# Four-quarter inverse products and an opening by token blocks in a hybrid mixer kernel

## The chip, the core and the metric

The kernel runs on one core of a Trainium2 chip. The metric is the device time of one execution in microseconds (us). A core has TensorE (PE: matmuls, with the weight loads shown apart as PEld), VectorE (DVE), ScalarE (ACT), GpSimd (POOL) and SyncE (SP, which here only issues DMAs). PE writes to PSUM, 8 banks of 512 fp32 numbers in each of 128 partitions.

## What is computed

One decoder layer over 512 tokens and 16 meta tokens, width 1024:

```python
h = (_rms(x, norm1_g[l]) * valid).astype(dt)
z = h @ w_in[l]
...
r, decay, k, v, kk, a, g = rwkv7_project(c_in, ...)
y_rw = rwkv7_mix(r, decay, k, v, kk, a, g, rw_rk[l], rw_ln_g[l], rw_ln_b[l])
...
merged = (gates[:, :, 0] * (y_sb.astype(dt) @ p_sb[l]) + ...)
x = x + (merged.astype(dt) @ w_o[l]).astype(dt)
h2 = _rms(x, norm2_g[l]).astype(dt)
x = x + squared_relu_mlp(h2, w_up[l], w_down[l]).astype(dt)
```

`rwkv7_mix` is a scan over the tokens, for 8 heads of 64 channels:

```python
S = (S * w_t[:, :, None, :]
     - jnp.einsum('bhij,bhj->bhi', S, kk_t)[..., None] * b_t[:, :, None, :]
     + v_t[..., None] * k_t[:, :, None, :])
```

## The kernel before

Every engine runs one hand-written program; semaphores order them (`wait_ge`, `then_inc`). Nothing is scheduled at run time.

**Dense work.** All large products are "jobs", in one list (`JOBS`). A job's weights come as units of 128 x 1024 numbers: SP loads a unit into `raw` (3 slots), ACT rounds it to the high part (`high`, `w_hi`, L784), POOL subtracts for the low part (`low`, `w_lo`, L667). The activations too are kept as high and low parts, and a product is three matmuls (`product3`, L1611 to L1613). A feature job over all 544 columns does them as two halves of 272 columns, for 8 slices `k` of the width each.

**Opening.** `x` arrives in four blocks of 128 tokens (`xt`) and the meta block (`xm`, 32 rows). ACT takes sums of squares and the scale of each block (L798 to L800), DVE multiplies by it (L1192). When all five blocks are scaled, PE turns them (L1650, L1653) for one slice `k` after the other, all blocks in a slice; ACT (L805, L806) and DVE (L1202, L1205) multiply the turned slice by the gain `norm1_g`, which lies along the partitions, and split it into `h_hi` and `h_lo`. Then the dense jobs begin, first the two of `PHASE_C[0]` and `PHASE_C[1]`; ACT copies the result of each (L820).

**RWKV part.** The scan is done for 32 meta tokens (block 0, one chunk of 32) and four blocks of 128 tokens, each two chunks of 64, whose rows stand in partitions 0 to 63 and 64 to 127. Within a chunk an inverse of a 64 x 64 triangle is built in 6 levels (5 in block 0) for each head. A level beyond the first is: PE `c1` products (L2055: `MM` by `TT`), ACT copy to `C1` (L1141), PE `u` products (L2064: `C1` by `XX`), DVE addition into `XX` (L1528), DVE transposition into `TT` (L1534); POOL masks the next `MM` (L744). Heads come in two groups `g` of four. Between `c1` and `u`, and between `u` and the next `c1`, PE does a piece of a dense job (`pieces(fill[...])`). After the levels come `F` products (L2073), their copy into `FK` (L1146), `wz` products (L2081), their copy (L1537) and the products of the state (L2096 to L2105); between these three `RW_FILL` has no pieces.

These products have 64 rows in and 64 out, so each uses one quarter of the PE array. The lines that say which:

```python
for h in range(4 * g, 4 * g + 4):
    o = CH * (h % 4)
    for rows, _, _ in chunks:
        last = M(pst[rows, 4 + 2 * g, o:o + m], MM[rows, step % 2, h, 0:m],
                 TT[rows, h, 0:m], start=True, stop=True)
```

The output partitions are the input's: chunk 0 uses the quarter (rows 0 to 63 in, 0 to 63 out), chunk 1 the one opposite. `c1` of group `g` goes to bank 4 + 2g, `u` to bank 5 + 2g. The products of the state (L2096 to L2105) already use all four quarters: either chunk's rows to either half of the output.

Of the kernel before, what the change touches and what calls it, by code (L numbers as in the profile page):

```python
# [6 lines left out]
ALU = mybir.AluOpType  # L7
ACT = mybir.ActivationFunctionType
# [5 lines left out]
P = 128  # L14
# [204 lines left out]
def build(nc, x, meta, weights, lora, consts, params, out):  # L219
    with ExitStack() as ctx:  # L220
# [35 lines left out]
        rs0 = place("rs0", [P, NB + 1], at=at)  # L256

# [146 lines left out]
        hn_ready = sem("hn_ready")  # L404
        ht_done = sem("ht_done")
# [3 lines left out]
        zeros_ready, cbuf_zeroed = sem("zeros_ready"), sem("cbuf_zeroed")  # L409
        c_copied, c_mixed = sem("c_copied"), sem("c_mixed")  # L410
        wa_tanh, sg_tanh, sg_ready = sem("wa_tanh"), sem("sg_tanh"), sem("sg_ready")
# [12 lines left out]
        f_done, f_copied, wz_done, wz_ready = sem("f_done"), sem("f_copied"), sem("wz_done"), sem("wz_ready")  # L424
# [17 lines left out]
        sb_diag_zeroed, sb_kmd_ready, sb_vmd_ready = sem("sb_diag_zeroed"), sem("sb_kmd_ready"), sem("sb_vmd_ready")  # L442
# [8 lines left out]
        rg_tanh, rqd_ready, rsz_zeroed = sem("rg_tanh"), sem("rqd_ready"), sem("rsz_zeroed")  # L451
# [38 lines left out]
        def halves(row):  # L490
            return row.rearrange("p (a b) -> p a b", a=2)

# [140 lines left out]
        def _(sp):  # L633
            for b in range(NB):
                if b == NB - 1:

                    sp.wait_ge(zeros_ready, 1)
                    sp.dma_start(xm[MB - N_META:MB, :], meta).then_inc(x_in, 16)
# [20 lines left out]
        def _(pool):  # L659
# [106 lines left out]
        def _(act):  # L766
# [36 lines left out]
            for k in range(KD):  # L803
# [3 lines left out]
                if k in (2, 4):  # L807
                    high(k // 2)
# [1394 lines left out]
```

## Time and profile before

| | |
|---|---|
| median of 3 runs | 1324.9 us (1324.51 to 1329.6) |
| the profiled execution's own time | 1325.9 us |
| its span in the profile | 1324.1 us |
| PE busy | 1234.7 us (93%) |
| chain that ended last | 77% PE |
| mean granted TensorE clock | 0.983 of full |

The profile shows one execution. A timeline row may merge several instructions of a line (xN), its duration then runs from the first's start to the last's end. A plain fp32 matmul leaves two records, so eight 64 x 64 products are 16 records.

### The profile page before, as it was taken

What the parts mean: (1) busy time and instruction counts of PE and PEld (TensorE: products, weight loads), DVE (VectorE), ACT (ScalarE), POOL (GpSimd) and SP (SyncE); (2) the same over time, 40 slices, a digit from 0 to 9 for tenths busy, and PEclk for the clock granted to TensorE, in tenths of its full rate; (3) what the DMA queues carried; (4) which work ended last, traced back from release to release, by engine and by line L of the source; (5) the groups of instructions that cost most, each with busy time, mean ns of one, the idle gap of its engine ahead of it and who ended that gap; (6) DMA issues with size and microseconds to landing.
All of it is one profiled execution on the core that took longest, in us unless ns stands there. A gap on an engine that the chain in (4) does not pass through costs nothing.

```text
span 1324.1 us, 21007 instructions
## 1 busy us (share of the span) xinstructions
PE 1234.7 (93%) x9042; PEld 1018.6 (77%) x9042; DVE 460.7 (35%) x834; ACT 492.7 (37%) x788; POOL 465.6 (35%) x287
## 2 busy tenths in 40 slices
PE   5999999899999989997999989888899999999998
PEld 4998878787889668765677767668788888788886
DVE  3599221323231452442243464453422200122000
ACT  5456322121222342776344543542533311133210
POOL 2443435232423224333232432233234544244541
PEclk9999999999999999999999999999999999999999
DMA  6212323121211132101421211141122232122330
GB/s 227 80 65 88 117 77 106 43 72 65 97 51 49 40 110 74 35 32 48 181 79 56 82 64 65 48 143 64 64 80 96 97 111 96 64 96 96 112 127 32
DMA packets 33340, 110.17 MB, mean 83 GB/s; under 512 B 4048, under 2 KB 6064, under 8 KB 32608
## 3 DMA queue, kind: packets, MB, share of 16 engines
q1 hardware_dynamic: 25952, 92.44, 21.1%
q10 hardware_dynamic: 6784, 16.26, 3.3%
q8 instruction: 72, 1.18, 0.4%
q0 software_dynamic: 512, 0.13, 0.0%
q14 instruction: 20, 0.16, 0.0%
HBM read 99.42 MB, written 9.04 MB: 82 GB/s over the span
## 4 chain that ended last, share of the span: by engine, by line
PE 77%; DVE 10%; ACT 6%; issue 3%; POOL 2%; DMA 1%; ACTq 0%; DVEq 0%; SPq 0%; POOLq 0%
PE pst L1611 17%; PE pst L1612 16%; PE pst L1613 16%; PE pst L1764 4%; PE pst L1766 4%; PE pst L1765 4%; PE pst L2064 2%; PE pst L2055 2%; PE pst L1803 1%; ACT w_hi L784 1%; DVE merged L1297 1%; PE pst L1790 1%; PE pst L1856 1%; PE pst L2081 1%; ACT gate_t L934 1%
## 5 line engine op out<-in xcount | busy, mean ns | idle before, releaser
L667 POOL TENSOR_TENSOR w_lo<-raw,w_hi 128x1024 fp32r<-128x1024 f32 x164 | 399.8, 2443 | 733.2 <-ACT w_hi L784 721.6
L1611 PE MATMUL pst<-h_hi,w_hi 128*128 128x512 f32 (+1 forms) x960 | 357.8, 373 | 4.2 <-DVE x L1316 2.6
L1612 PE MATMUL pst<-h_lo,w_hi 128*128 128x512 f32 (+1 forms) x960 | 346.0, 360 | 0.0
L1613 PE MATMUL pst<-h_hi,w_lo 128*128 128x512 f32 (+1 forms) x960 | 345.9, 360 | 0.0
L784 ACT ACTIVATE w_hi<-raw 128x1024 fp32r<-128x1024 f32 x164 | 171.2, 1050 | 147.4 <-PE pst L1766 114.3
L1611 PEld LDWEIGHTS pst<-h_hi,w_hi 128*128 128x128 f32 x960 | 182.7, 190 | 40.2 <-issue 5.6
L1612 PEld LDWEIGHTS pst<-h_lo,w_hi 128*128 128x128 f32 x960 | 183.0, 191 | 27.4 <-issue 2.2
L1613 PEld LDWEIGHTS pst<-h_hi,w_lo 128*128 128x128 f32 x960 | 182.6, 190 | 27.6
L1611 PE MATMUL pst<-w_hi,h_hi 128*128 128x256 f32 (+3 forms) x328 | 94.9, 290 | 6.8 <-DVE h_lo L1483 3.7
L1766 PE MATMUL pst<-w_hi,u_lo 128*128 128x512 f32 x256 | 99.6, 389 | 0.0
L1764 PE MATMUL pst<-w_hi,u_hi 128*128 128x512 f32 x256 | 99.6, 389 | 0.0
L1765 PE MATMUL pst<-w_lo,u_hi 128*128 128x512 f32 x256 | 99.6, 389 | 0.0
L1612 PE MATMUL pst<-w_lo,h_hi 128*128 128x256 f32 (+3 forms) x328 | 93.1, 285 | 0.0
L1613 PE MATMUL pst<-w_hi,h_lo 128*128 128x256 f32 (+3 forms) x328 | 92.7, 283 | 0.0
L890 ACT ACTIVATE stage<-pst 128x512 f32<-128x512 f32 (+5 forms) x36 | 17.8, 495 | 164.2 <-PE pst L1613 164.2
L1307 DVE TENSOR_TENSOR usq<-ub 128x512 f32<-128x512 f32 x32 | 22.9, 715 | 138.8 <-ACT ub L940 138.8
L1528 DVE TENSOR_TENSOR rw_x<-rw_x,pst 128x256 f32<-128x256 f32 (+1 forms) x48 | 18.3, 382 | 146.8 <-PE pst L2064 146.3
L1611 PEld LDWEIGHTS pst<-w_hi,h_hi 128*128 128x128 f32 (+1 forms) x328 | 60.4, 184 | 9.6 <-DVE h_lo L1483 4.1
L1316 DVE TENSOR_TENSOR x<-pst,x 128x512 f32<-128x512 f32 x16 | 9.9, 684 | 165.1 <-PE pst L1766 165.1
L940 ACT ACTIVATE ub<-pst 128x512 f32<-128x512 f32 x32 | 19.2, 599 | 122.1 <-PE pst L1613 122.1
L1612 PEld LDWEIGHTS pst<-w_lo,h_hi 128*128 128x128 f32 (+1 forms) x328 | 60.5, 184 | 0.4 <-issue 0.2
L1613 PEld LDWEIGHTS pst<-w_hi,h_lo 128*128 128x128 f32 (+1 forms) x328 | 60.6, 185 | 0.2
(324 smaller groups left out, 1738.0 us busy)
## 6 DMA issues: line engine op xcount, KB each, us to landing
raw<-in_weights SPq DMA_DIRECT2D x164, 512.0 KB, 3.4
xt<-in_x SPq DMA_DIRECT2D x4, 512.0 KB, 5.5
wait_gate<-stage ACTq DMA_DIRECT2D x8, 256.0 KB, 2.0
gate_t<-wait_gate ACTq DMA_DIRECT2D x1, 2048.0 KB, 8.3
x<-in_x ACTq DMA_DIRECT2D x1, 2048.0 KB, 8.9
out<-x SPq DMA_DIRECT2D x8, 256.0 KB, 3.3
cst<-in_consts SPq DMA_DIRECT2D x1, 1524.0 KB, 10.6
wait_ret_v<-stage ACTq DMA_DIRECT2D x8, 128.0 KB, 2.0
```

What stands on the lines that cost most here:

```text
L667: nc.gpsimd.tensor_tensor(w_lo[:, u % W_SLOTS, :], raw[:, u % RAW_SLOTS, :], w_hi[:, u % W_SLOTS, :].bitcast(F32), ALU.subtract).then_inc( ...
L784: nc.scalar.activation(w_hi[:, u % W_SLOTS, :], raw[:, u % RAW_SLOTS, :], ACT.Copy)\
L940: A(ub[:, i % 2, :], one, ACT.Relu).then_inc(job_out[kind], 1)
L1307: link(V.tensor_tensor(q, r, r, ALU.mult))
L1611: M(out, lh, rh, start=(first and i == 0), stop=False)
L1612: M(out, lh, rl, start=False, stop=False)
L1613: last = M(out, ll, rh, start=False, stop=(final and i == len(terms) - 1))
L1764: M(o, u_hi[:, f, toks], w_hi[:, us, ws], start=(f == 0), stop=False)
L1765: M(o, u_hi[:, f, toks], w_lo[:, us, ws], start=False, stop=False)
L1766: last = M(o, u_lo[:, f, toks], w_hi[:, us, ws], start=False, stop=(f == FH - 1))
L2055: last = M(pst[rows, 4 + 2 * g, o:o + m], MM[rows, step % 2, h, 0:m], TT[rows, h, 0:m], start=True, stop=True)
L2064: last = M(pst[rows, 5 + 2 * g, o:o + m], C1[rows, h, 0:m], XX[rows, h, 0:m], start=True, stop=True)
```

## The change

It has two parts.

**Four quarters.** For the odd heads `c1`, `u`, `F` and `wz` products now write to the other half of the partitions (`turned`, `out_rows_of`), and go to bank 5 + 2g; the even heads' go to bank 4 + 2g (`places` gives the order). In each bank `c1` (and `F`) stands from column 0 on, `u` (and `wz`) from column 256 on. What reads the results has to move the odd heads' halves back: one instruction for the even heads over all 128 partitions and two for the odd heads over 64 each (`by_parity`), in place of one for the group. The copy of `F` and that of `wz` are shared anew: ACT has `F` of group 0 and `wz` of group 1, DVE `F` of group 1 and `wz` of group 0.

**Opening.** The gain is spread over the partitions by two matmuls (a row of ones by the gain's row, its own small DMA on ACT's queue), and DVE multiplies it in before the turning (L1192 becomes a product of three). Blocks 0, meta and 1 are turned first, each on its own; then comes the first half (272 columns) of the first dense job, then the turning of blocks 2 and 3, then the first half of the second job and the second halves of both. SP loads in another order, the first weight unit before the last two token blocks.

```diff
+        TOKEN_ORDER = [0, NB, 1, 2, 3]
+        def h_bank(b, half):
+            return [2, 4, 4, 6][b] + half
+        def h_parts(b):
+            if b == NB:
+                return [(pst[:, 1, 0:KD * MB].rearrange("p (k c) -> p k c", k=KD), (slice(0, KD), slice(0, MB)), 3)]
+            cols, n = slice(MB + P * b, MB + P * b + P), [1, 4, 6, 8][b]
+            return [(pst[:, h_bank(b, i), :].rearrange("p (k c) -> p k c", k=4), (slice(4 * i, 4 * i + 4), cols), n + i)
+                    for i in range(2)]
...
+        def turned(b):
+            if b == 0:
+                return [(slice(0, MB), slice(0, MB))]
+            return [(slice(CH * i, CH * i + CH), slice(CH - CH * i, P - CH * i)) for i in range(2)]
+        def by_parity(b, g):
+            h0, every = 4 * g, slice(0, rw_blocks[b][0])
+            return [(every, every, slice(h0, h0 + 4, 2), 4 + 2 * g)] + \
+                   [(to, at_, slice(h0 + 1, h0 + 4, 2), 5 + 2 * g) for to, at_ in turned(b)]
+        def two(row):
+            return row.rearrange("p (h d) -> p h d", h=2)
+        def out_rows_of(b, h):
+            return [at_ if h % 2 else to for to, at_ in turned(b)]
...
+            token_block(0)
+            sp.dma_start(cst[:, 0:P], consts[:, 0:P]).then_inc(turn_in, 16)
+            sp.wait_ge(zeros_ready, 2)
+            sp.dma_start(xm[MB - N_META:MB, :], meta).then_inc(x_in, 16)
+            token_block(1)
+            weight_unit(0)
+            token_block(2)
+            token_block(3)
             sp.dma_start(par[:], params).then_inc(const_in, 16)
-            sp.dma_start(cst[:, 0:P], consts[:, 0:P]).then_inc(const_in, 16)
-            for u in range(NU):
-                if u >= RAW_SLOTS:
-                    sp.wait_ge(lo_ready, u - RAW_SLOTS + 1)
-                sp.dma_start(raw[:, u % RAW_SLOTS, :], weights[u]).then_inc(raw_in[u % RAW_SLOTS], 16)
-                if u == 0:
-                    sp.dma_start(cst[:, P:NCONST], consts[:, P:NCONST]).then_inc(table_in, 16)
-                    sp.dma_start(lor[:], lora).then_inc(table_in, 16)
+            for u in range(1, RAW_SLOTS):
+                weight_unit(u)
...
+            act.dma_start(gain_row[:], gain).then_inc(turn_in, 16)
...
+            def token_high(b):
+                for src, dst, n in h_parts(b):
+                    act.wait_ge(ht_done, n + 1)
+                    A(h_hi[:, dst[0], dst[1]], src, ACT.Copy).then_inc(hhi_ready, 1)
+            token_scale(0)
+            token_scale(NB)
+            token_scale(1)
+            high(1)
+            token_high(0)
+            token_high(NB)
+            token_high(1)
+            token_scale(2)
+            token_scale(3)
+            high(2)
+            token_high(2)
+            token_high(3)
             high(RAW_SLOTS)
...
-                        A(C1[0:n, 4 * g:4 * g + 4, 0:m], four(pst[0:n, 4 + 2 * g, 0:256])[:, :, 0:m], ACT.Copy)\
-                            .then_inc(c1_copied[g], 1)
+                        for to, at_, hs, bank in by_parity(b, g):
+                            last = A(C1[to, hs, 0:m], two(pst[at_, bank, 0:128])[:, :, 0:m], ACT.Copy)
+                        last.then_inc(c1_copied[g], 1)
                     pieces(fill["c1"][l] + fill["tu"][l])
-                for g in range(2):
-                    act.wait_ge(f_done, 2 * b + g + 1)
-                    A(FK[0:n, 4 * g:4 * g + 4, 1, :], four(pst[0:n, 4 + 2 * g, 0:256]), ACT.Copy).then_inc(f_copied, 1)
+                act.wait_ge(f_done, 2 * b + 1)
+                for to, at_, hs, bank in by_parity(b, 0):
+                    last = A(FK[to, hs, 1, :], two(pst[at_, bank, 0:128]), ACT.Copy)
+                last.then_inc(f_copied[0], 1)
+                act.wait_ge(wz_done, 2 * b + 2)
+                for to, at_, hs, bank in by_parity(b, 1):
+                    last = A(FK[to, hs, :, :], pst[at_, bank, 256:512].rearrange("p (h a d) -> p h a d", h=2, a=2),
+                             ACT.Copy)
+                last.then_inc(wz_ready[1], 1)
...
+                V.scalar_tensor_tensor(out=halves(src), in0=halves(src), scalar=rs0[0:r, b:b + 1], in1=pst[0:r, 6:8, :],
+                                       op0=ALU.mult, op1=ALU.mult).then_inc(hn_ready, 1)
+            def token_low(b):
+                for src, dst, n in h_parts(b):
+                    dve.wait_ge(hhi_ready, n)
+                    V.tensor_tensor(h_lo[:, dst[0], dst[1]], src, h_hi[:, dst[0], dst[1]].bitcast(F32), ALU.subtract)\
+                        .then_inc(hlo_ready, 1)
+            dve.wait_ge(ht_done, 1)
+            token_norm(0)
+            token_norm(NB)
+            token_norm(1)
+            token_low(0)
+            token_low(NB)
+            token_low(1)
+            token_norm(2)
+            token_norm(3)
+            token_low(2)
+            token_low(3)
...
-                            V.tensor_tensor(XX[0:n, hs, 0:m], XX[0:n, hs, 0:m],
-                                            four(pst[0:n, 5 + 2 * g, 0:256])[:, :, 0:m], ALU.add).then_inc(added, 1)
+                            for to, at_, hp, bank in by_parity(b, g):
+                                last = V.tensor_tensor(XX[to, hp, 0:m], XX[to, hp, 0:m],
+                                                       two(pst[at_, bank, 256:384])[:, :, 0:m], ALU.add)
+                            last.then_inc(added, 1)
...
+                dve.wait_ge(f_done, 2 * b + 2)
+                for to, at_, hs, bank in by_parity(b, 1):
+                    last = V.tensor_copy(FK[to, hs, 1, :], two(pst[at_, bank, 0:128]))
+                last.then_inc(f_copied[1], 1)
+                dve.wait_ge(wz_done, 2 * b + 1)
+                for to, at_, hs, bank in by_parity(b, 0):
+                    last = V.tensor_copy(FK[to, hs, :, :],
+                                         pst[at_, bank, 256:512].rearrange("p (h a d) -> p h a d", h=2, a=2))
+                last.then_inc(wz_ready[0], 1)
...
+            pe.wait_ge(zeros_ready, 1)
+            pe.wait_ge(turn_in, 32)
+            for i in range(2):
+                last = M(pst[:, 6 + i, :], ones_row[:], gain_row[:, T * i:T * i + T], start=True, stop=True)
+            last.then_inc(ht_done, 1)
+            def token_turn(b):
+                pe.wait_ge(hn_ready, TOKEN_ORDER.index(b) + 1)
+                for k in range(KD):
+                    if b == NB:
+                        last = nc.tensor.transpose(pst[:, 1, MB * k:MB * k + MB], xm[:, P * k:P * k + P],
+                                                   cst[0:MB, 0:MB])
+                    else:
+                        last = nc.tensor.transpose(pst[:, h_bank(b, k // 4), P * (k % 4):P * (k % 4) + P],
+                                                   xt[:, b, P * k:P * k + P], ident)
+                    if k == KD - 1 or k == 3 and b < NB:
+                        last.then_inc(ht_done, 1)
+            for b in (0, NB, 1):
+                token_turn(b)
+            feature_job(PHASE_C[0], ALL, 0, 2)
+            token_turn(2)
+            token_turn(3)
+            feature_job(PHASE_C[1], ALL, 0, 2)
+            feature_job(PHASE_C[0], ALL, 1, 2)
+            feature_job(PHASE_C[1], ALL, 1, 2)
...
-            feature_job(PHASE_C[0], ALL)
-            feature_job(PHASE_C[1], ALL)
...
+            def places(b, g):
+                return [(rows, out_rows_of(b, h)[ci], h) for t in (2 * g, 2 * g + 1)
+                        for ci, (rows, _, _) in enumerate(chunks_of(b)) for h in (2 * t, 2 * t + 1)]
...
-                        for h in range(4 * g, 4 * g + 4):
-                            o = CH * (h % 4)
-                            for rows, _, _ in chunks:
-                                last = M(pst[rows, 4 + 2 * g, o:o + m], MM[rows, step % 2, h, 0:m],
-                                         TT[rows, h, 0:m], start=True, stop=True)
+                        for rows, out_rows, h in places(b, g):
+                            o = CH * (h % 4 // 2)
+                            last = M(pst[out_rows, 4 + 2 * g + h % 2, o:o + m], MM[rows, step % 2, h, 0:m],
+                                     TT[rows, h, 0:m], start=True, stop=True)
                         last.then_inc(c1_done[g], 1)
```

On PE's order this shows at two places. Before, from the start of the program (names: `cst` holds the identity, `xt` and `xm` the tokens):

```order
L1650 MATMUL pst<-cst,xt 128x128 x4
L1653 MATMUL pst<-cst,xm 128x32
L1650 MATMUL pst<-cst,xt 128x128 x4
L1653 MATMUL pst<-cst,xm 128x32
L1650 MATMUL pst<-cst,xt 128x128 x4
```

That pair stands eight times, and then the dense jobs begin. Of the change, from the start of the program (`gain_row` and `ones_row` hold the gain and the ones):

```order
L1726 MATMUL pst<-gain_row,ones_row 128x512 x2
L1736 MATMUL pst<-cst,xt 128x128 x8
L1733 MATMUL pst<-cst,xm 128x32 x8
L1736 MATMUL pst<-cst,xt 128x128 x8
L1690 MATMUL pst<-h_hi,w_hi 128x272
L1691 MATMUL pst<-h_lo,w_hi 128x272
L1692 MATMUL pst<-h_hi,w_lo 128x272
```

and, where those 24 dense matmuls end:

```order
L1692 MATMUL pst<-h_hi,w_lo 128x272
L1736 MATMUL pst<-cst,xt 128x128 x16
L1690 MATMUL pst<-h_hi,w_hi 128x272
```

The same 32 turnings of `xt` and 8 of `xm` stand there, 16 of them behind 24 dense ones that need only the first columns.

DVE at the end of the levels of blocks 1 to 4 (the additions of the last level, then the copies into `FK`, which the order calls `rw_wz`), before:

```order
L1534 STREAM_TRANSPOSE rw_t<-rw_x 128x256
L1528 TENSOR_TENSOR rw_x<-rw_x,pst 128x256 x2
L1537 COPY rw_wz<-pst 128x512 x2
```

and of the change, from the second group's additions on:

```order
L1601 TENSOR_TENSOR rw_x<-rw_x,pst 128x2x64
L1601 TENSOR_TENSOR rw_x<-rw_x,pst 64x2x64 x2
L1611 COPY rw_wz<-pst 128x2x64
L1611 COPY rw_wz<-pst 64x2x64 x2
L1615 COPY rw_wz<-pst 128x2x128
L1615 COPY rw_wz<-pst 64x2x128 x2
```

Each addition of 128 x 256 (here, and in every level beyond the first) became three of 128 columns, and DVE took over a part of the `F` copy; ACT's copies to `C1` were split in the same way.

## Rows read from the trace of the kernel before

**Rows 1.** The page: busy time and share by engine; the chain that ended last.
```profile
PE 1234.7 (93%) x9042; PEld 1018.6 (77%) x9042; DVE 460.7 (35%) x834; ACT 492.7 (37%) x788; POOL 465.6 (35%) x287
...
PE 77%; DVE 10%; ACT 6%; issue 3%; POOL 2%; DMA 1%; ACTq 0%; DVEq 0%; SPq 0%; POOLq 0%
```

**Rows 2.** PE waits: line, whom it waited for, us in total, times, longest.
```profile
PE pst L1650 <- DVE xt L1192: 14.0, 1, 14.0
...
PE pst L2055 <- POOL rw_m L744: 5.1, 5, 4.4
```

**Rows 3.** Timeline of the opening, ACT, DVE and POOL: start, duration, line, operation.
```profile
4.28 1.06 ACT L798 ACTIVATE sq<-xt 128x1024 f32<-128x1024 f32 x1 [2.18 <-DMA xt<-in_x]
...
13.09 0.75 DVE L1192 TENSOR_SCALAR xt<-xt,rs 128x1024 f32<-128x1024 f32 x1 [0.77 <-ACT rs L800]
...
16.31 0.75 DVE L1202 SCALAR_TENSOR_TENSOR h_lo<-pst,par,h_hi 128x512 fp32r<-128x512 f32 x1 [2.27 <-ACT h_hi L806]
...
18.68 1.06 ACT L784 ACTIVATE w_hi<-raw 128x1024 fp32r<-128x1024 f32 x1
...
19.82 2.36 POOL L667 TENSOR_TENSOR w_lo<-raw,w_hi 128x1024 fp32r<-128x1024 f32 x1 [18.07 <-ACT w_hi L784]
...
39.01 0.63 ACT L820 ACTIVATE cbuf<-pst 128x544 f32<-128x544 f32 x1 [4.39 <-PE pst L1613]
```

**Rows 4.** Timeline of the opening, PE: the first turned tiles.
```profile
13.98 1.09 PE L1650 MATMUL pst<-cst,xt 128*128 128x128 f32 x4 [13.98 <-DVE xt L1192]
...
15.00 0.31 PE L1653 MATMUL pst<-cst,xm 32*128 32x32 f32 x1
```

**Rows 5.** Stretches of the first two dense jobs: us, PE busy (instructions), clock, DMA.
```profile
24.30:29.50 5.20, 5.20 (x24) 1.00 0.40 147
29.50:38.90 9.40, 9.40 (x76) 1.00 0.24 65
```

**Rows 6.** Timeline of one inverse level, all engines.
```profile
208.84 1.15 PE L2064 MATMUL pst<-rw_x,rw_c 64*64 64x64 f32 x32
...
209.57 0.42 DVE L1528 TENSOR_TENSOR rw_x<-rw_x,pst 128x256 f32<-128x256 f32 x1 [6.43 <-PE pst L2064]
...
210.81 0.45 DVE L1534 STREAM_TRANSPOSE rw_t<-rw_x 128x256 f32<-128x256 f32 x1
...
212.90 1.15 PE L2055 MATMUL pst<-rw_t,rw_m 64*64 64x64 f32 x32
...
213.98 0.50 PE L1611 MATMUL pst<-h_hi,w_hi 128*128 128x512 f32 x1
...
214.45 0.65 ACT L1141 ACTIVATE rw_c<-pst 128x256 f32<-128x256 f32 x2
```

**Rows 7.** Timeline of the state products after the inverse.
```profile
240.64 0.34 PE L2096 MATMUL pst<-rw_scores,rw_wz 64*64 64x64 f32 x8
...
240.80 0.30 PE L2099 MATMUL pst<-rw_b_tok,rw_wz 64*64 64x64 f32 x8
...
242.66 0.39 PE L1611 MATMUL pst<-w_hi,h_hi 128*128 128x256 f32 x1
```

**Rows 8.** Timeline of a block's tail: `F`, its copy, the first product behind `wz`.
```profile
307.44 1.15 PE L2073 MATMUL pst<-rw_v_tok,rw_scores 64*64 64x64 f32 x32
...
308.16 0.85 ACT L1146 ACTIVATE rw_wz<-pst 128x256 f32<-128x256 f32 x2 [3.14 <-PE pst L2073]
...
310.55 0.34 PE L2096 MATMUL pst<-rw_scores,rw_wz 64*64 64x64 f32 x8
```

**Rows 9.** Groups by line and shape: busy us, mean ns; idle before, releaser.
```profile
L2055 PE MATMUL pst<-rw_t,rw_m 64*64 64x64 f32 x640 | 24.4, 226 | 5.1 <-POOL rw_m L744 5.1
...
L1551 DVE TENSOR_TENSOR rw_kappa_r<-rw_kappa_r,pst 128x128 f32<-128x128 f32 x16 | 4.5, 280 | 1.9 <-PE pst L2105 1.9
...
L2151 PE MATMUL pst<-rw_kappa_r,cst 128*128 128x512 f32 x8 | 4.2, 605 | 0.5 <-ACT rw_kappa_r L1152 0.5
```

**Rows 10.** One stretch: us, busy of PE, PEld, DVE, ACT, POOL, clock, DMA.
```profile
180.00:190.00 10.00, 8.36 (x100) 7.32 (x101) 3.95 (x8) 1.34 (x3) 2.04 (x1) 0.83 0.21 64
```

More of the change, by code:

```diff
@@ L216, with build @@
 SBUF_BASE, SBUF_END = 16512, 229344
-def build(nc, x, meta, weights, lora, consts, params, out):
+def build(nc, x, meta, weights, lora, consts, params, gain, out):
     with ExitStack() as ctx:
@@ L256, in build @@
         rs0 = place("rs0", [P, NB + 1], at=at)
+        gain_row = place("gain_row", [1, D], at=at)
+        ones_row = place("ones_row", [1, P], at=at)
         at = [region]
@@ L404, in build @@
         hn_ready = sem("hn_ready")
+        turn_in = sem("turn_in")
         ht_done = sem("ht_done")
@@ L792, in _, with token_scale @@
             A = nc.scalar.activation
+            act.dma_start(gain_row[:], gain).then_inc(turn_in, 16)
             nc.scalar.preload_act_table_set("natural_log_exp_and_others")
-            for b in list(range(NB - 1)) + [NB, NB - 1]:
+            def token_scale(b):
                 r, src = (P, xt[:, b, :]) if b < NB else (MB, xm[:])
@@ L800, in _ @@
                 A(rs0[0:r, b:b + 1], rs0[0:r, b:b + 1], ACT.Exp, scale=-0.5).then_inc(rs_ready, 1)
[L802 to L808 removed]
+            def token_high(b):
[14 more added lines that the diff above has]
+            token_high(3)
             high(RAW_SLOTS)
             nc.scalar.preload_act_table_set("exp_and_others")
[L813 removed]
+            act.wait_ge(par_ready, 4)
             def c_copy(i):
@@ L2060, in _ @@
                         pe.wait_ge(c1_copied[g], step - b)
-                        for h in range(4 * g, 4 * g + 4):
-                            o = CH * (h % 4)
-                            for rows, _, _ in chunks:
-                                last = M(pst[rows, 5 + 2 * g, o:o + m], C1[rows, h, 0:m], XX[rows, h, 0:m],
-                                         start=True, stop=True)
+                        for rows, out_rows, h in places(b, g):
+                            o = 256 + CH * (h % 4 // 2)
+                            last = M(pst[out_rows, 4 + 2 * g + h % 2, o:o + m], C1[rows, h, 0:m], XX[rows, h, 0:m],
+                                     start=True, stop=True)
                         last.then_inc(u_done[g], 1)
@@ L2070, in _ @@
                     pe.wait_ge(x_ready[g], level0[b] + levels_of[b])
-                    for h in range(4 * g, 4 * g + 4):
-                        for rows, _, _ in chunks:
-                            last = M(pst[rows, 4 + 2 * g, HD * (h % 4):HD * (h % 4) + HD], AM[rows, h, 0, 0:m],
-                                     VT[rows, HD * h:HD * h + HD], start=True, stop=True)
+                    for rows, out_rows, h in places(b, g):
+                        o = HD * (h % 4 // 2)
+                        last = M(pst[out_rows, 4 + 2 * g + h % 2, o:o + HD], AM[rows, h, 0, 0:m],
+                                 VT[rows, HD * h:HD * h + HD], start=True, stop=True)
                     last.then_inc(f_done, 1)
@@ L2077, in _ @@
                 for g in range(2):
-                    pe.wait_ge(f_copied, 2 * b + g + 1)
-                    for h in range(4 * g, 4 * g + 4):
-                        for rows, _, _ in chunks:
-                            last = M(pst[rows, 5 + 2 * g, P * (h % 4):P * (h % 4) + P].rearrange("p (a d) -> p a d", a=2),
-                                     XX[rows, h, 0:m], FK[rows, h, :, :], start=True, stop=True)
+                    pe.wait_ge(f_copied[g], b + 1)
+                    for rows, out_rows, h in places(b, g):
+                        o = 256 + P * (h % 4 // 2)
+                        last = M(pst[out_rows, 4 + 2 * g + h % 2, o:o + P].rearrange("p (a d) -> p a d", a=2),
+                                 XX[rows, h, 0:m], FK[rows, h, :, :], start=True, stop=True)
                     last.then_inc(wz_done, 1)
```

87 lines of the change are left out of this document (32 added, 55 removed).

## The prediction

> **What bounds the kernel now.** I read the page first. PE is busy 93% of the span and holds 77% of the chain that ended last; every other engine is near 35% [rows 1]. So time is won where PE starts sooner or does the same work in less, and a slower evacuation costs only where PE comes to wait for it. The list of PE's waits says where it waits: 14.0 us once, before the first turned tile, and then 5.1 us for POOL's masks, 4.4 of them at one place [rows 2]. The timeline of the opening shows what the 14.0 us are: the first scale could start at 4.28, but the last block is scaled only at 13.09 [rows 3], and PE turns nothing before that. The timeline of one inverse level shows PE without a gap: products, dense piece, products [rows 6].
>
> PE does not run at its higher clock at first. 24 dense matmuls of 272 columns take 5.20 us, 0.217 each; later 76 take 9.40, 0.124 each [rows 5]. The clock column prints 1.00 for both; the pace says that the first stretch was at the lower of the two levels (1.2 GHz).
>
> **Part 1: the four quarters.** A batch of `c1` or `u` (both groups, 16 products, 32 records) starts at 212.90 and the dense piece behind it at 213.98: 1.08 us of PE [rows 6]. Its products use two opposite quarters. The state products have the same shape and use all four: 16 groups of 8 records from 240.64 to 242.66, 2.02 us for 128 records [rows 7]. Less about 0.15 for leaving the shape, that is 14.6 ns a record. 32 such records take 0.47, and with the same 0.10 for leaving 0.57: a batch gives back 0.51 us. Blocks 1 to 4 have five levels with both batches: 4 x 5 x 2 = 40 batches (640 records of L2055 are 20 batches [rows 9]), **20.4 us**. Block 0 has one chunk, so `turned` changes nothing there: 0.
>
> Here the trace contradicts a rule. The Trainium skill (TensorE: Matmul & The Clock Gate, "Wait — 56ns, not 53.3ns?") says that start-to-start of matmuls never falls below about 25 ns, however few columns they have. By it the state products could not run at 14.6 ns a record, and they do [rows 7]. By that rule a batch would take 0.90 and the sum would be 7 us in place of 20.4.
>
> Is the longer evacuation hidden? `u` starts at 208.84, DVE adds at 209.57, its last transposition ends at 211.26, and the next `c1` starts at 212.90 [rows 6]: 1.6 us to spare. After: PE leaves 0.5 us less. An addition of 128 columns takes 0.28 alone [rows 9] and, by my estimate, 0.2 where the next is queued behind it, so three take 0.68 in place of 0.42; the two groups add 0.5, and the first group's products end 0.25 sooner. The spare is about 0.85 us. ACT's copy of `C1` ends at 215.10 and `u` begins at 216.96 (one level took 4.06) [rows 6]; six short copies in place of two add about 0.4 of that 1.9. Cost: 0. Without this cover, each 0.1 us of lateness would cost 2 us over 20 gaps. POOL's masks are not touched, and the 4.4 us stays.
>
> The tail of a block has no pieces for cover. `F` starts at 307.44, ACT copies from 308.16, and the state products begin at 310.55, 3.11 us later [rows 8]. The new chain: `F` of group 0 done at 0.35, ACT ready 0.5, three copies to 1.1, `wz` of group 0 to 1.7, DVE's three copies of 256 columns 1.1 us, start at 2.9 to 3.0. PE's 1.4 us less of work turns into waiting: 0.1 to 0.3 us a block, **0.6 us** for all (0 to 2).
>
> **Part 2: the opening.** I walk the new chain with the durations of before.
> - Block 0 lands at 4.28 as now [rows 3]; the identity is right behind it, say 4.6. The two gain matmuls: 8 records of a 128 x 512 plain fp32 product take 4.2 us, so 1.05 a product at full pace [rows 9] and some 1.8 at the low one: ready at 8.4. This is later than the scale of block 0 and gates DVE.
> - DVE's product of three reads PSUM: 0.75 for 512 columns [rows 3], so 1.25 for 1024. Blocks 0, meta, 1: 9.7, 11.0, 12.3.
> - PE: four turnings take 1.02 [rows 4], so eight 2.1; block 0 9.8 to 11.9, meta (8 small ones, about 1.5) to 13.4, block 1 to 15.5.
> - ACT's high half and DVE's low half of a bank are 0.7 each: the first half of the first job can start at about 16.1. Its weights (ACT 1.06, POOL 2.36 [rows 3]) are ready by 12.5.
> - 24 matmuls at 0.217 to 21.4; by then the clock should rise, as it did 5.2 us into the dense work before. 16 turnings 1.8 to 23.3. ACT scales blocks 2 and 3 behind block 1's copies, until 19.5, and DVE follows: in time. The second weight unit is ready at about 23. Then 72 matmuls at 0.124: 9.0, to 32.3.
>
> Before, the second job ended just ahead of ACT's copy at 39.01 [rows 3], at 38.8. **6.5 us** sooner. Bounds: if the turnings and half of the rest stay at the lower clock, +2.4 and +2.2, which leaves 2; if the gain, the turning and the wait for weights come 2 us sooner, 8.5. SP's queue: the large constant table now stands behind two weight units, by bytes some 3 us later, and is wanted only behind the second job.
>
> Sum: 20.4 + 0.6 + 6.5 = 27.5. The profiled execution took 1325.9, so 1298.4; the median of the runs is 1.0 lower. I take **1297**.
>
> **The rivals.**
> - *The clock falls more often (1303).* In 180 to 190 the granted clock is 0.83 [rows 10], the lower level for 3.4 us, which gives away 1.7 us; and PE is busy 8.36 of the 10 us there. The new tails of blocks 1 to 4 hold about 1.5 us of waiting where PE was full. One such fall in each: 6.8 us. Against: no fall shows in the mean of 0.983 beyond some ten of these in the whole span, and PE still works through half of each tail. 0.13.
> - *Two row halves in one bank do not run together (1318.5).* The Trainium skill (TensorEngine Tiling (Array Packing), "Gotcha 1: PSUM Pressure") forbids different row tiles the same bank at the same time. In the state products each bank belongs to one chunk's rows; the new code writes both chunks' rows into each bank. If that holds them at two at a time, part 1 gives 0 and only 6.5 remain. Against: before, both chunks wrote one bank too, in 31 ns a record, and four quarters over two banks at 14.6 are twice that pace [rows 6, 7], so two banks in turn should do. 0.06.
> - *The 25 ns floor holds for this order (1311).* Against it the 14.6 ns [rows 7]. 0.03.
> - *The opening brings nothing (1304).* The gain matmuls or the wait at block 1 take more, or the clock falls again while PE alternates. 0.08.
> - *Slower (1337).* DVE's and ACT's reads that move data between partition halves, which no row shows, are slow. It decides where DVE's chain is 1.4 us late in each of 20 gaps, which eats 27.5: additions of 0.6 us in place of 0.2. At 0.7 the chain is 2.0 late, 40 us, and with 27.5 gained the time is 1337. 0.03.
> - *As forecast (1297, own range 1291 to 1303).* 0.67.
>
> **How the numbers follow.** The range 1290 to 1309 takes in the forecast, the clock and the opening rivals (0.88) and leaves out most of the rest. Measurements of this kernel tell 0.5% (6.6 us) from no change. Faster by more than that means under 1318.3: the forecast, clock, opening and floor cases and half of the bank case, 0.94. Within 0.5%: 0.03. Slower: 0.03.
>
> **What would show it.** In the profile after: the first dense matmul at about 16 and the copy of the second job's result near 32.5; a `c1` or `u` batch of 32 records in 0.6 us in place of 1.15, still with no PE wait for DVE's additions or ACT's copies; about 3.0 us from `F` to the state products, now with PE waiting for the copies; the 4.4 us wait for POOL unchanged. Wrong if batches still take over 1 us, if PE waits for `XX` or `C1`, or if the granted clock falls in the tails.

## The result and the profile after

| | before | after |
|---|---|---|
| median of 4 runs each, us | 1326.9 (1324.5 to 1329.6) | 1312.3 (1308.7 to 1315.3) |
| ratio, 95% interval | | 0.9875 (0.9846 to 0.9904) |
| profiled execution, us (span) | 1325.9 (1324.1) | 1310.0 (1307.8) |
| mean granted clock of it | 0.983 | 0.977 |

The change made the kernel 14.6 us shorter. The forecast said 1297, with 1290 to 1309, so the time lies 3 us above the range. In a second comparison (below) the ratio was 0.9856. Line numbers moved: `c1` L2055 is now L2151, `u` L2064 is L2159, `F` L2168, `wz` L2176, the state products L2191 to L2200, ACT's copies L1198 (`C1`), L1203 (`F`) and L1207 (`wz`), DVE's addition L1601 and copies L1611 and L1615, POOL's mask L789, the dense matmuls L1690 to L1692.

The page, busy time by engine and the chain that ended last:

```profile
PE 1217.1 (93%) x9046; PEld 999.2 (76%) x9046; DVE 485.3 (37%) x933; ACT 515.4 (39%) x887; POOL 465.3 (36%) x288
...
PE 76%; DVE 11%; ACT 6%; issue 3%; POOL 2%; DMA 1%; ACTq 0%; DVEq 0%; SPq 0%; POOLq 0%
```

PE is still the bound at 93%; DVE and ACT carry about 100 instructions more each [rows 1].

The waits of PE (us in total, times, longest):

```profile
PE pst L2151 <- POOL rw_m L789: 6.1, 6, 4.4
...
PE pst L2176 <- ACT rw_wz L1203: 5.5, 5, 1.7
...
PE pst L1726 <- DMA cst<-in_consts: 4.8, 1, 4.8
...
PE pst L2191 <- DVE rw_wz L1615: 3.9, 4, 1.0
```

The 14.0 us in front of the first turned tile are gone [rows 2]. In their place PE waits 4.8 us for the identity's transfer, 1.4 for the first scaled block and 0.65 for the first low half. Two waits in the tails, for the copies of `F` and of `wz`, are longer or new.

The opening, timeline, against [rows 3 to 5]:

```profile
4.77 3.75 PE L1726 MATMUL pst<-gain_row,ones_row 1*128 1x512 f32 x4 [4.77 <-DMA cst<-in_consts]
...
8.56 1.28 DVE L1255 SCALAR_TENSOR_TENSOR xt<-xt,rs,pst 128x1024 f32<-128x1024 f32 x1 [8.56 <-PE pst L1726]
...
9.89 1.97 PE L1736 MATMUL pst<-cst,xt 128*128 128x128 f32 x8 [1.37 <-DVE xt L1255]
...
10.95 1.26 DVE L1255 SCALAR_TENSOR_TENSOR xt<-xt,rs,pst 128x1024 f32<-128x1024 f32 x1
...
15.40 0.56 PE L1690 MATMUL pst<-h_hi,w_hi 128*128 128x272 f32 x1 [0.65 <-DVE h_lo L1261]
...
31.53 0.63 ACT L876 ACTIVATE cbuf<-pst 128x544 f32<-128x544 f32 x1 [1.37 <-PE pst L1692]
```

The copy of the second job's result moved from 39.01 to 31.53, 7.5 us.

The level of an inverse in front of the one in [rows 6] (its last line is the `u` batch with which [rows 6] begins):

```profile
194.51 0.89 DVE L1601 TENSOR_TENSOR rw_x<-rw_x,pst 128x128 f32<-128x128 f32 x3 [4.08 <-PE pst L2159]
...
197.59 0.69 PE L2151 MATMUL pst<-rw_t,rw_m 64*64 64x64 f32 x32
198.21 0.50 PE L1690 MATMUL pst<-h_hi,w_hi 128*128 128x512 f32 x1
...
199.14 1.70 ACT L1198 ACTIVATE rw_c<-pst 128x128 f32<-128x128 f32 x6
...
201.19 0.69 PE L2159 MATMUL pst<-rw_x,rw_c 64*64 64x64 f32 x32
201.82 0.50 PE L1690 MATMUL pst<-h_hi,w_hi 128*128 128x512 f32 x1
```

A batch takes 0.63 us to the next dense matmul (201.19 to 201.82), where it took 1.08. Three additions take 0.89, six copies 1.70: about 0.28 each, as long as one that stands alone (0.28 in [rows 9]), so queued ones do not get shorter here.

The tail of block 3 (in [rows 8] it is block 2's), before:

```profile
371.12 1.15 PE L2073 MATMUL pst<-rw_v_tok,rw_scores 64*64 64x64 f32 x32
...
373.55 1.50 DVE L1537 COPY rw_wz<-pst 128x512 f32<-128x512 f32 x2 [4.65 <-PE pst L2081]
...
374.30 0.34 PE L2096 MATMUL pst<-rw_scores,rw_wz 64*64 64x64 f32 x8
```

and after:

```profile
353.84 0.69 PE L2168 MATMUL pst<-rw_v_tok,rw_scores 64*64 64x64 f32 x32
...
354.66 0.84 ACT L1203 ACTIVATE rw_wz<-pst 128x128 f32<-128x128 f32 x3 [0.44 <-PE pst L2168]
...
355.56 1.10 PE L2176 MATMUL pst<-rw_wz,rw_x 64*64 64x128 f32 x32 [1.02 <-ACT rw_wz L1203]
356.29 1.29 DVE L1615 COPY rw_wz<-pst 128x256 f32<-128x256 f32 x3 [0.73 <-PE pst L2176]
...
357.64 0.34 PE L2191 MATMUL pst<-rw_scores,rw_wz 64*64 64x64 f32 x8 [0.98 <-DVE rw_wz L1615]
```

PE waits twice for about 1 us. From `F` to the state products it is 3.80 us, where it was 3.18. DVE begins to copy `wz` as long behind `F` as before (2.45 us, before 2.43), so PE's faster products gained nothing up to there. Then its three copies of 256 columns take 1.29, where PE needed only the first of two copies of 512 columns (0.69).

Where the time went, by the starts of PE's products in the two traces. "Clock held" takes out half of the time that PE worked at the lower of its two levels (1.2 GHz), behind the moment at which the clock first rose (29.6 us before, 20.0 after). It takes out too much where PE would have waited anyway:

| stretch | before | after | clock held |
|---|---|---|---|
| start to the first turned RWKV tile | 138.60 | 131.04 | -7.6 |
| first `c1` to `F`, block 1 | 41.11 | 36.80 | -4.3 |
| block 2 | 42.28 | 38.25 | -3.9 |
| block 3 | 39.89 | 36.52 | -3.4 |
| block 4 | 42.83 | 38.51 | -4.3 |
| `F` to the state products, blocks 1 to 4 in sum | 13.50 | 15.70 | +2.2 |
| between these stretches, in sum (block 0 is here) | 131.8 | 133.6 | -1.6 |
| behind the RWKV blocks (same code in both) | 874.2 | 877.4 | +0.4 |

The last row is the striking one: 3.2 us were lost where nothing was changed. The granted clock says why. PE was at the lower level for 47 us of the span before and for 62 after. The row above it has more of this, too: in block 0 the lower level lasts twice as long (6.8 us against 3.4), and right behind the tail of block 3 there is a fall where none was. In a second record of the changed kernel block 0 has no more of the lower level than before, and from its first `c1` to that of block 1 it takes 47.11 us against 47.08: the change costs nothing there, as forecast.

### The profile page after: what moved, and what is told of

Its sections match the earlier page's. It is cut to its first block, busy times and chain, and to the rows that moved or that the text cites. A ratio compares the mean times of both kernels' runs of the same rounds, so it can differ in the third digit from the quotient of the medians.

```text
span 1307.8 us, 21215 instructions
## 1 busy us (share of the span) xinstructions
PE 1217.1 (93%) x9046; PEld 999.2 (76%) x9046; DVE 485.3 (37%) x933; ACT 515.4 (39%) x887; POOL 465.3 (36%) x288
## 4 chain that ended last, share of the span: by engine, by line
PE 76%; DVE 11%; ACT 6%; issue 3%; POOL 2%; DMA 1%; ACTq 0%; DVEq 0%; SPq 0%; POOLq 0%
PE pst L1690 17%; PE pst L1691 16%; PE pst L1692 16%; PE pst L1858 4%; PE pst L1857 4%; PE pst L1856 4%; PE pst L2159 1%; PE pst L2151 1%; ACT w_hi L829 1%; DMA sw_v<-wait_sw_v 1%; PE pst L1895 1%; DVE merged L1369 1%; PE pst L1882 1%; PE pst L1948 1%; POOL rw_m L789 1%
## 5 line engine op out<-in xcount | busy, mean ns | idle before, releaser
L1690 PE MATMUL pst<-h_hi,w_hi 128*128 128x512 f32 (+1 forms) x960 | 358.1, 373 | 4.8 <-DVE x L1388 2.6
L1692 PE MATMUL pst<-h_hi,w_lo 128*128 128x512 f32 (+1 forms) x960 | 345.7, 360 | 0.0
L1690 PEld LDWEIGHTS pst<-h_hi,w_hi 128*128 128x128 f32 x960 | 182.9, 190 | 41.5 <-issue 6.9
L1692 PEld LDWEIGHTS pst<-h_hi,w_lo 128*128 128x128 f32 x960 | 182.5, 190 | 27.7
L1690 PE MATMUL pst<-w_hi,h_hi 128*128 128x256 f32 (+3 forms) x328 | 95.2, 291 | 6.8 <-DVE h_lo L1555 3.6
L1692 PE MATMUL pst<-w_hi,h_lo 128*128 128x256 f32 (+3 forms) x328 | 92.7, 284 | 0.0
L1601 DVE TENSOR_TENSOR rw_x<-rw_x,pst 64x128 f32<-64x128 f32 (+1 forms) x136 | 36.4, 272 | 116.6 <-PE pst L2159 115.3
L1690 PEld LDWEIGHTS pst<-w_hi,h_hi 128*128 128x128 f32 (+1 forms) x328 | 60.6, 185 | 9.6 <-DVE h_lo L1555 4.1
L1692 PEld LDWEIGHTS pst<-w_hi,h_lo 128*128 128x128 f32 (+1 forms) x328 | 61.0, 186 | 0.2
L789 POOL TENSOR_TENSOR rw_m<-rw_scores,cst 128x256 f32<-128x256 f32 (+1 forms) x58 | 39.6, 704 | 60.1 <-DVE rw_scores L1582 48.3
```

The costliest lines, as they stand in the source:

```text
L789: nc.gpsimd.tensor_tensor(MM[0:n, step % 2, 4 * g:4 * g + 4, 0:m], AM[0:n, 4 * g:4 * g + 4, 2, 0:m], C("levels", CH * l, CH * l + m, n).un ...
L1601: last = V.tensor_tensor(XX[to, hp, 0:m], XX[to, hp, 0:m], two(pst[at_, bank, 256:384])[:, :, 0:m], ALU.add)
L1690: M(out, lh, rh, start=(first and i == 0), stop=False)
L1692: last = M(out, ll, rh, start=False, stop=(final and i == len(terms) - 1))
```

## The experiments

Theory: the quarters bring some 16 us and the opening 7.5; the copies in three pieces cost 2 in the tails; the clock takes a part of the rest. Rivals: the gain is one of banks and not of quarters; the gain ahead is handed back in more falls of the clock. Each ratio is to the kernel before on the same chip; four kernels at a time share the 11 to 17 runs of before beside them. The medians of before are 1329.9 (the first four), 1331.7 and 1329.2 us in the three groups, so kernels of different groups are best compared by their ratios.

### The parts by themselves

The opening alone keeps the old products: `four(pst[0:n, 4 + 2 * g, 0:256])`, one copy for a group.

> The opening of the changed kernel alone; the inverse's products stay in two quarters. In the trace of the changed kernel the first turning of the receptance stands 7.56 us sooner than before. Theory A (the two parts add, and each shows the time that its stage shows): 7.5 us less than before, ratio about 0.9943. Rival B (the time gained ahead moves the later work into more stretches of half clock, whatever gains it): only 2 to 5 us are left at the end, ratio 0.996 to 0.9985, with more time at half clock than the 47.3 us of the record before. Rival C (the opening is given back in the prepared stage): under 2 us.

1322.1 us, ratio 0.9945 (0.9926 to 0.9964): 7.3 us. The first turned RWKV tile is at 131.47. Theory A, though the record has 54 us at the lower level against 47; the forecast's term was 6.5.

The quarters alone, with the old opening.

> The inverse's products, F and the solutions in four quarters; the opening of before. Counted from the trace of the changed kernel: levels 16.0 us gained over four blocks, tails 2.2 to 2.8 lost, block 0 some 1.0 lost. Theory A (these sizes are the whole of it): 12 to 13 us less than before, ratio about 0.9905. Rival B (a part of the gain is lost in half-clock stretches that the new timing brings): 6 to 9 us less, ratio about 0.9945, and over 55 us at half clock in its record. The forecast's own size would be 21 us, ratio 0.984.

1317.4 us, 0.9908 (0.9883 to 0.9932): 12.2 us. Theory A by the time, though its record shows 72 us at the lower level, as B said. With the clock held, its RWKV stretches shrink as those of the changed kernel: 4.3, 4.3, 3.4 and 4.3 us of levels, tails 2.2 us longer in sum. The parts add: 7.3 + 12.2 = 19.5, and the whole change gave 19.2 beside them:

> The changed kernel once more, for its spread beside the others on one chip and for a second record of its half-clock stretches. Theory A (the stretches belong to the program's own timing): stretches at the same places as in the first record (173.6, 358.0, 603.7, 747 us from the span's start) and about 61 us in sum, ratio 0.985 to 0.990 to before. Rival B (they fall at random over the executions): other places, and a sum anywhere between 45 and 65 us.

1310.7 us, 0.9856 (0.9829 to 0.9883). Its record has 58 us at the lower level. Most falls stand at the same places within 2 us (254, 356, 472, 606, 749, 885, 937), but two of the first record are gone (689, 829), two are shorter, one is longer, and two are new (421, 630). So A for the places where PE waits long, B for the rest: which of the smaller waits costs a fall differs between executions. The times of one kernel spread with it: by 5 us in the five runs here and 13 in the 43 of before.

Levels in quarters, tails as before:

```diff
-                    for rows, out_rows, h in places(b, g):
-                        o = HD * (h % 4 // 2)
-                        last = M(pst[out_rows, 4 + 2 * g + h % 2, o:o + HD], AM[rows, h, 0, 0:m],
+                    for h in range(4 * g, 4 * g + 4):
+                        for rows, _, _ in chunks:
+                            last = M(pst[rows, 4 + 2 * g, HD * (h % 4):HD * (h % 4) + HD], AM[rows, h, 0, 0:m],
```

> The changed kernel with F and the solutions in the old scheme of two quarters and one copy for a group; the products of the levels stay in four quarters. Theory A (the copies in three pieces lengthen every tail from F to the state products by 0.55 us and block 0's by about 1): 2.5 to 3.5 us less than the changed kernel, the stretch from the first F to the first state product back at 3.1 to 3.9 us. Rival B (the tails got longer by the clock and the pieces beside them, not by the copies): the same time as the changed kernel within 1 us, tails at 3.5 to 4.5 us.

1312.2 us, 0.9869 (0.9845 to 0.9893): no gain over the changed kernel (1310.7 beside it), as B said. But its trace shows the tails as A said:

```profile
352.99 1.15 PE L2155 MATMUL pst<-rw_v_tok,rw_scores 64*64 64x64 f32 x32
...
354.24 1.96 PE L2163 MATMUL pst<-rw_wz,rw_x 64*64 64x128 f32 x32
355.45 1.50 DVE L1603 COPY rw_wz<-pst 128x512 f32<-128x512 f32 x2 [4.20 <-PE pst L2163]
356.19 0.34 PE L2178 MATMUL pst<-rw_scores,rw_wz 64*64 64x64 f32 x8
```

3.20 us from `F` to the state products against 3.80. What it gained there it lost to the clock: 0.972 in the mean of its runs, 78 us at the lower level in its record. Why this version has more falls is not shown.

### Quarters or banks?

```diff
-            return [(slice(CH * i, CH * i + CH), slice(CH - CH * i, P - CH * i)) for i in range(2)]
+            return [(slice(CH * i, CH * i + CH), slice(CH * i, CH * i + CH)) for i in range(2)]
```

> The changed kernel with the rows of odd heads not turned: banks by parity of the head, copies and additions in three pieces, both as in the change, but only two of TensorE's four quarters are used, as before. It prices the copies apart from the quarters. Theory A (the four quarters carry the gain of the levels, about 0.5 us for a batch of two sets of products, and the three-piece copies cost little of it): 16 to 20 us slower than the changed kernel, that is 2 to 4 us slower than the opening alone, near 1325 us. Rival C (the banks by parity bring the gain, not the quarters): near the changed kernel, 1311 us. Rival D (the copies cost as much as the quarters gain and something else gains): under 8 us slower than the changed kernel.

1328.9 us, 0.9983 (0.9962 to 1.0004), with before at 1331.7. Theory A: without the turned rows nothing is left of the RWKV gain, although banks, copies and additions are those of the change. A batch:

```profile
201.04 1.20 PE L2159 MATMUL pst<-rw_x,rw_c 64*64 64x64 f32 x32
202.16 0.50 PE L1690 MATMUL pst<-h_hi,w_hi 128*128 128x512 f32 x1
```

1.12 us against 1.08 before and 0.63 with four quarters. From first `c1` to `F` block 1 takes 41.62, against 41.11 before and 36.80 after. So the quarters give 4.8 us a block, and the scheme around them takes back 0.5. In the four tails together it is 16.7 us, against 13.5 before and 15.7 after: the copies in three pieces cost 3.2 there, and four quarters give back 1.0.

### The clock

If PE's waits make the clock fall, work in the waits should hold it. Products of the identity, never read, stand ahead of some 25 waits, in a bank that nobody reads at that time:

```diff
+            def warm(count, bank=None, col=3 * P):
+                if count and bank is None:
+                    n, part, _ = PIECES[piece[0]]
+                    bank = 2 * job_slot(n) + (n < JOB_NO[("av", 0, 0)])
+                    if part == 0:
+                        pe.wait_ge(*emptied(n - 2))
...
+                for _ in range(count):
+                    M(pst[:, bank, col:col + P], ident, ident, start=True, stop=True)
...
+                    warm([3, 3, 2, 3, 5][b] if g == 0 else 0)
                     pe.wait_ge(f_copied[g], b + 1)
```

> The changed kernel with idle products of the identity (128x128, results never read) ahead of some 25 waits of TensorE, three to twenty-four in each, counted to take about two thirds of the wait: in the receptance blocks (tok waits, F, solutions, the mask wait of 4.35 us) and behind them (waits of 1.1 to 7.3 us). Theory A (the clock falls because TensorE waited for much of a stretch; the change makes such waits more frequent and so pays a part of its gain): time at half clock falls from about 60 us to 25 or less, and the kernel gets 8 to 18 us shorter than the changed kernel. Rival B (the falls follow the chip's own state, not TensorE's waits): as much time at half clock as without, and the same time or 1 to 5 us more for fillers that run past their wait.

1302.0 us, 0.9781 (0.9756 to 0.9807), granted clock 0.991 in the mean of its runs. Three stretches of the changed kernel (us, busy PE, PEld, DVE, ACT, POOL, clock, DMA):

```profile
470.00:480.00 10.00, 6.94 (x45) 6.95 (x46) 2.72 (x5) 2.61 (x4) 2.38 (x1) 0.83 0.51 203
745.00:755.00 10.00, 7.52 (x26) 6.09 (x27) 6.10 (x16) 5.09 (x13) 4.74 (x2) 0.66 0.30 97
935.00:950.00 15.00, 10.04 (x36) 7.96 (x36) 7.51 (x26) 6.79 (x25) 0.00 (x0) 0.66 0.01 2
```

and of this one:

```profile
470.00:480.00 10.00, 9.09 (x66) 7.93 (x66) 2.46 (x6) 1.81 (x4) 2.39 (x1) 1.00 0.42 162
745.00:755.00 10.00, 8.31 (x47) 6.61 (x46) 7.30 (x17) 4.96 (x15) 4.80 (x2) 1.00 0.31 105
935.00:950.00 15.00, 13.48 (x68) 11.05 (x67) 6.06 (x19) 7.21 (x20) 3.58 (x2) 1.00 0.02 3
```

PE is busier and the clock is full. In sum 25 us at the lower level instead of 58 to 62. By the ratios the gain over the changed kernel is 10 us, by the medians 8.7. Theory A for most falls: they come from PE's waits. In the record of the changed kernel 11 of the 12 falls begin during a wait of 1 to 7.4 us or within 2 us of its end; the twelfth, at 173.6, stands in block 0, behind a wait of 0.93 and small products. Counted the other way round, that record has 33 waits of 0.98 us and more behind the opening: all ten of 2 us and more have a fall with them, and one of the 23 shorter ones. In the record of before it is eight of ten and one of 16. The fall in block 0 is the exception: it stays in all three kernels with idle products in that tail (at 175.3, 181.0 and 173.1 us, for 6.8 to 10.2 us), so what brings it is not shown. The Trainium skill (TensorE: Matmul & The Clock Gate, "HAM oscillation — how this bites in real kernels") says that gaps in PE's work bring the lower clock back, and the trace agrees; but the gap that the page names is longer than most waits that stand ahead of a fall here (1.0, 2.3 and 2.6 us among them).

> The same idle products in the kernel of before (fewer in the tails, whose waits are shorter there). Theory A: time at half clock from 47 us to under 25, 6 to 13 us less than before; and the distance from this kernel to the changed one with idle products is the change's worth without the clock, 21 to 24 us, against the 15 to 19 us measured with it. Rival B: no change of the time at half clock; the distance stays at 15 to 19 us.

1322.6 us, 0.9935 (0.9911 to 0.9959). Theory A for the clock. From here to 1302.0 it is **20.6 us**: the change's worth with the clock held, just under what A said. It isn't quite clean, for the idle products ran past some of their waits. Block 1's tail in this kernel:

```profile
237.40 1.15 PE L2097 MATMUL pst<-rw_v_tok,rw_scores 64*64 64x64 f32 x32
...
240.62 0.49 PE L1619 MATMUL pst<-cst 128*128 128x128 f32 x2
241.04 0.34 PE L2122 MATMUL pst<-rw_scores,rw_wz 64*64 64x64 f32 x8
```

That is 3.64 us from `F` to the state products, where it took 3.28 without idle products; the four tails lose 1.4 us so, and those of the changed kernel nothing. In the tail of block 0 the idle products lengthen the changed kernel by about 1 us more than this one. The two nearly cancel, and the worth is some 20 us.

> The same idle products in the version with F and the solutions in the old scheme (levels in four quarters, new opening), whose record had 78 us at half clock and, per mean clock times span, 4 us less work than the changed kernel. Theory A: with the clock held it is the fastest of all, 3 to 5 us under the changed kernel with idle products, near 1292 to 1298 us. Rival B: 1312 us as without them.

1301.1 us, 0.9782 (0.9758 to 0.9807): B's 1312 is refuted, but it lies 0.9 us under the changed kernel with idle products, not 3 to 5. The idle products in its tails, too, had run past their waits (3.64 us in block 1, 3.28 without them).

### The terms of the opening

```diff
-            act.dma_start(gain_row[:], gain).then_inc(turn_in, 16)
+            act.dma_start(gain_row[:], gain).then_inc(gain_in, 16)
...
-            pe.wait_ge(turn_in, 32)
+            pe.wait_ge(gain_in, 16)
```

> The changed kernel, but the products that spread the gain row wait for the gain row alone and no longer for the identity's transfer, which ended their wait at 4.77 us. Theory A (the opening is a chain: gain products 3.7 us, scaling, turning, so it moves as a whole): the scaling of the first block moves from 8.56 to about 7, held next by the row factor of ScalarE at 6.1, and the first dense product from 15.4 to 13.6 to 14.4; 1.0 to 1.8 us less than the changed kernel, if the weights are in. Rival E (gain row and identity land together, or weights and the low halves of POOL hold the first dense product): no change within 0.5 us.

1307.5 us, 0.9848 (0.9822 to 0.9873), before at 1329.2.

```profile
2.78 3.74 PE L1726 MATMUL pst<-gain_row,ones_row 1*128 1x512 f32 x4 [2.78 <-DMA gain_row<-in_gain]
...
6.57 1.28 DVE L1255 SCALAR_TENSOR_TENSOR xt<-xt,rs,pst 128x1024 f32<-128x1024 f32 x1 [6.57 <-PE pst L1726]
```

The first dense product starts at 13.47, the first turned RWKV tile at 128.97: 2.1 us sooner. The chain moves as a whole, as A said. The ratio shows 1.1 of it, within the noise of the clock.

```diff
-            feature_job(PHASE_C[0], ALL, 0, 2)
             token_turn(2)
             token_turn(3)
-            feature_job(PHASE_C[1], ALL, 0, 2)
-            feature_job(PHASE_C[0], ALL, 1, 2)
-            feature_job(PHASE_C[1], ALL, 1, 2)
+            feature_job(PHASE_C[0], ALL)
+            feature_job(PHASE_C[1], ALL)
```

> The changed kernel with all five turnings ahead of the first dense job and both jobs done whole, token blocks kept. Theory A (doing the first halves around the last turnings hides the scaling and splitting of blocks 2 and 3): the first dense product starts at about 22 instead of 15.4 us and the second job ends at 35 to 37 instead of 31.5; 4 to 5 us slower than the changed kernel, so 3 of the 7.5 us stay with the block order and the gain row. Rival F (the order by token blocks brings it all): within 1 us of the changed kernel.

1314.2 us, 0.989 (0.9862 to 0.9918).

```profile
18.21 3.68 PE L1736 MATMUL pst<-cst,xt 128*128 128x128 f32 x16 [3.51 <-DVE xt L1255]
21.54 0.57 PE L1690 MATMUL pst<-h_hi,w_hi 128*128 128x272 f32 x1
```

PE stands idle for 3.51 us where the first halves were. The first turned RWKV tile is at 134.65, 3.6 us later. Theory A by the traces. By the ratios it is 2.0 to 4.5 us slower than the changed kernel, whichever of its two comparisons is taken. So of the opening's 7.3 to 7.6 us the halves are about half.

### A version that beats both

Levels in quarters, old tails, early gain and idle products, without those that had run past their waits:

> A version put together from the runs: levels in four quarters, F and the solutions in the old scheme, new opening with the early gain, idle products in the waits (without those that had made TensorE wait for a bank at 653 us and in the tails). Theory A: 1296 to 1300 us, under all so far; time at half clock under 30 us. Rival B (the clock's gain does not add to it): 1305 or more.

1294.8 us, **0.9747** (0.9721 to 0.9773). Theory A, and 1.2 us under the range that it named: 34 us under before, some 15 under the changed kernel by the ratios (0.9856).

> The same with the tails of the changed kernel (F and solutions in four quarters, copies in three pieces) in place of the old ones. Theory A (per block from F to the state products the three-piece copies cost 0.4 to 0.6 us, 2.2 us in four blocks, once the clock is held): 1.5 to 2.5 us slower than the version with the old tails. Rival G (tails are no dearer): equal within 0.5 us.

1296.7 us, 0.9762 (0.9735 to 0.9788). The difference of 2.0 us has A's sign and size, and the traces have the tails at 3.28 and 3.88 us in block 1; the intervals overlap, so it is shown by the traces and not by the times. The two also differ in their idle products (23 more in the tails here), and the profiled execution with the old tails, which had one fall more (at 251.9), was the longer by 0.7 us.

All results of a group in one bank, which might have spared a copy, weren't tried: two row halves would then write the same half of a bank at once, and no run here shows what that does.

## Why the prediction was wrong

The mechanisms held for the batches and the opening; the sizes of two terms did not, and one of them had the wrong sign. 27.5 us were forecast. 14.6 and 19.2 were measured, and some 20 with the clock held.

- **"a batch gives back 0.51 us ... 20.4 us".** This is the step that failed most. The levels gave 15.9 us in this trace (16.3 in the pair with idle products). The pace of a record was as forecast, and four quarters against two in the same scheme gave 0.49 a batch (1.12 to 0.63). But a batch that changes bank with each head is 0.04 longer even in two quarters. Leaving the shape was set at 0.10; with 32 records at 14.6 ns it is 0.16. And the shorter batches lost cover. In a block's first `c1` the second group waits 0.40 for POOL's mask, where it waited 0.19 or nothing, so that batch went from 1.48 to 1.26 (in block 2 from 1.91 to 1.50). In block 3 `u` waits for ACT's copies behind a short piece:

```profile
349.75 0.46 PE L2159 MATMUL pst<-rw_x,rw_c 64*64 64x64 f32 x16 [0.21 <-ACT rw_c L1198]
350.62 0.46 PE L2159 MATMUL pst<-rw_x,rw_c 64*64 64x64 f32 x16 [0.41 <-ACT rw_c L1198]
```

  Together: 35 undisturbed batches at 0.45 are 15.8; the first ones give 3 x 0.22 + 0.41; block 3 loses 0.18 + 0.21. That is 16.4, by which the pair with idle products (16.3) is explained, and the trace's 15.9 within the reading of its slow stretches.
- **"Cost: 0" for the longer evacuation.** Right for the full pieces, where DVE and ACT are ready in time, though a queued addition takes 0.28 and not 0.2. Wrong only at the short piece of block 3. The rival in which DVE is late did not come.
- **"0.6 us for all" in the tails.** Wrong in sign: 2.2 us were lost. The walk had `F` to state products at 2.9 to 3.0; it was 3.51 to 4.52 (before, 3.11 to 3.92, of which [rows 8] shows the shortest). Block 2, step by step against the walk: ACT is ready at 0.53 (0.5), its three copies take 0.84 (0.6), `wz` of group 0 takes 0.7 (0.6), and DVE's three copies take 1.29 (1.1). The copies are the cause: each is 0.28 for 128 columns and 0.43 for 256, and DVE's three stand wholly in PE's way, where one of 0.69 stood before.
- **Part 2, "6.5 us".** Right in mechanism and in nearly every time: gain at 8.5 (8.4), first dense product at 15.4 (16.1), second job done near 31.5 (32.3). The size was 7.3 to 7.6. A part of it is the moment at which the clock first rose: in the pair with idle products (27.4 and 21.7 us, against 29.6 and 20.0) block 0's first `c1` comes 5.6 us sooner, not 7.6.
- **Banks and the 25 ns floor.** Both rivals fell: a batch in four quarters takes 0.63 us, 14.6 ns a record, while both row halves write into each bank (into different halves of its partitions).
- **"The clock falls more often (1303)".** It came, at 0.13, beside the rest, and mostly elsewhere than it said: of four tails one has a fall, and most of what was added stands behind the RWKV blocks and in block 0. One record lost 14 us more at the lower level than the record before, some 5 to 6 of time. Over runs it is less: (1 - clock) times span is 28.8 in 43 runs of before and 31.6 in 9 of the changed kernel, and in the runs of before one such us costs 0.69. So about 2 us on average; in the first comparison, with 32.8, more. What else parts that comparison (14.6) from the second (19.2) is the spread of few runs; 3.0 of the 4.6 us are on the side of before (1326.9 against 1329.9).

Sum: 27.5 less 4.5 (levels), 2.8 (tails), plus 1 (opening) is 21.2, against some 20 with the clock held; the 1 us that is left is less than what the moment of the first rise moved (5.6 or 7.6 us). Less 1 to 6 for the clock, as runs fall, is the 15 to 19 that was measured. So the range was missed by three things at once: the batch, the tails, and in the first comparison the clock. By this sum the first two alone would have left the time inside it.

## What to carry over

An evacuation cut into pieces costs more in sum: DVE takes 0.28 us for 128 columns, 0.42 for 256 and 0.69 for 512, one copy behind the other. Where dense work covers it that is nothing, and in a tail without cover it eats what the faster products gave, so use the faster form only where there is cover. A gain in PE's busy time turns partly into waits, and waits of PE, nearly always when they are 2 us and more, cost the clock, also in code that was never changed: compare the granted clock of both records first, and try idle products in the waits, which were worth some 9 us here to either kernel.

## What was not expected of the hardware

- 392 more matmul records (196 idle products, never read) made the program 8.7 to 10 us faster by holding the granted clock at 0.991 in place of 0.977.
- Which of the shorter waits bring a fall differs from one execution to the next, and so do the times: within the 43 runs of before, the clock runs from 0.974 to 0.985 and the time from 1321 to 1335 us.
- The moment at which the clock first rises varies as well (18.5 and 20.0 us in two records of the changed kernel), and the first turned RWKV tile with it.
